# GpSimd's low halves of the weights in instructions of 256 elements per partition

## What is computed

```python
def trunk_layer(x, cvec, p, lam_init, ctx):
    shift1, scale1, gate1, shift2, scale2, gate2 = modulation(cvec, p['w_ada'], p['b_ada'])
    h = rms_norm(x, p['norm1_w']) * (1 + scale1) + shift1
    (mq, mk, mv, mo, mg, nq, nk, nv, dq, dk, dv, sz, sxbc, sdt, gpre) = split_cols(h @ p['w_in'])
    ...
    br = jnp.stack([a_out, b_out, c_out, d_out], axis=2)
    gates = jax.nn.sigmoid(gpre.reshape(B, S, N_BRANCH, D_MODEL))
    mixed = jnp.sum(gates * jnp.einsum('bsnc,ncd->bsnd', br, p['w_branch']), axis=2)
    x = x + gate1 * (mixed @ p['w_out'])
    h2 = rms_norm(x, p['norm2_w']) * (1 + scale2) + shift2
    x = x + gate2 * expert_choice_ffn(h2, p['w_router'], p['w_gate'], p['w_up'], p['w_down'])
```

## Time and profile before

| what | us |
|---|---|
| timed runs | 2199.38, 2208.94, 2211.12 |
| their median | 2208.94 |
| the profiled execution | 2198.71 |
| its span, first to last instruction | 2196.9 |
| GpSimd busy, 234 instructions | 455.8 |
| of that the low halves of L610, 164 instructions | 364.8 |
| VectorE busy, 1239 instructions | 662.9 |
| TensorE matmuls, 9096 | 1831.2 |

### The profile page before, as it was taken

One profiled execution on the slowest core, in us unless ns is written; L12 is line 12 of the kernel. 1 busy time (PEld: TensorE's weight loads), 2 busy tenths in 40 slices (PEclk: granted clock), 3 DMA queues, 4 the chain that ended last, 5 costly groups with the idle time before them and its releaser, 6 DMA issues.

```text
span 2196.9 us, 21970 instructions
## 1 busy us (share of the span) xinstructions
PE 1831.2 (83%) x9096; PEld 1169.9 (53%) x9096; DVE 662.9 (30%) x1239; ACT 545.7 (25%) x1054; POOL 455.8 (21%) x234
## 2 busy tenths in 40 slices
PE   5995988988988788888879879899686977888887
PEld 2885877877742222222358767777685422222223
DVE  2065334558320001011144452446584000110111
ACT  4432333221431111011144323322123310111111
POOL 0645322326200000000045452223271000000000
PEclk8998988978999999999989988889798999999999
DMA  9435243235479999999963424324323699999996
GB/s 353 106 115 197 99 147 114 99 97 186 157 305 407 428 425 427 428 427 428 394 195 119 153 108 142 132 91 163 108 87 153 260 429 427 427 428 429 427 427 293
DMA packets 119650, 567.72 MB, mean 258 GB/s; under 512 B 21376, under 2 KB 30848, under 8 KB 94464
## 3 DMA queue, kind: packets, MB, share of 16 engines
q1 hardware_dynamic: 108768, 543.91, 62.3%
q10 hardware_dynamic: 9920, 20.84, 2.7%
q0 software_dynamic: 864, 1.58, 0.3%
HBM read 550.57 MB, written 15.73 MB: 258 GB/s over the span
## 4 chain that ended last, share of the span: by engine, by line
PE 43%; DMA 35%; DVE 14%; ACT 3%; POOL 2%; issue 2%; SPq 1%; ACTq 0%; DVEq 0%
PE banks L678 19%; DMA ring<-in_w_down 11%; PE banks L1177 10%; DMA ring<-in_w_gate 10%; DMA ring<-in_w_up 10%; PE banks L995 2%; DVE work L1706 2%; DMA ring<-in_w_branch 1%; POOL small L624 1%; PE banks L684 1%; DMA ring<-in_w_ada 1%; DMA ring<-in_w_in 1%; PE banks L1147 1%; ACT work L1274 1%; DVE work L2075 1%
## 5 line engine op out<-in xcount | busy, mean ns | idle before, releaser
L1177 PE MATMUL banks<-ring,work 128*64 128x512 f32 x3072 | 703.3, 601 | 161.8 <-DMA ring<-in_w_gate 67.4
L610 POOL TENSOR_TENSOR ring_fp32r<-ring,ring_fp32r 128x1024 fp32r<-128x1024 f32 (+1 forms) x164 | 364.8, 2237 | 961.3 <-ACT ring_fp32r L1274 961.2
L1177 PEld LDWEIGHTS banks<-ring,work 128*64 128x64 f32 x3072 | 211.9, 137 | 615.8 <-issue 338.5
L678 PE MATMUL banks<-xT_fp32r,ring_fp32r 128*128 128x384 f32 x1280 | 367.9, 361 | 35.9 <-POOL ring_fp32r L610 32.6
L1274 ACT ACTIVATE work<-banks 32x512 f32<-32x512 f32 (+6 forms) x404 | 205.1, 528 | 458.4 <-PE banks L1177 253.4
L678 PEld LDWEIGHTS banks<-xT_fp32r,ring_fp32r 128*128 128x128 f32 x1280 | 251.0, 202 | 48.3 <-issue 39.1
L678 PE MATMUL banks<-hT_fp32r,ring_fp32r 128*128 128x384 f32 x640 | 225.4, 352 | 0.0
L1274 ACT ACTIVATE ring_fp32r<-ring 128x1024 fp32r<-128x1024 f32 (+1 forms) x164 | 156.4, 971 | 227.7 <-PE banks L678 161.9
L2129 DVE SCALAR_TENSOR_TENSOR xT<-banks,mod,xT 128x128 f32<-128x128 f32 (+1 forms) x128 | 46.9, 413 | 446.3 <-PE banks L1211 445.9
L678 PE MATMUL banks<-work_fp32r,ring_fp32r 128*128 128x384 f32 x768 | 149.1, 354 | 21.4 <-DVE work L2073 14.5
L678 PEld LDWEIGHTS banks<-work_fp32r,ring_fp32r 128*128 128x128 f32 x768 | 141.1, 198 | 27.6 <-DVE work L2073 11.4
(11 more groups left out here) (279 smaller groups left out, 1653.7 us busy)
## 6 DMA issues: line engine op xcount, KB each, us to landing
ring<-in_w_gate SPq DMA_DIRECT2D x64, 2048.0 KB, 12.2
ring<-in_w_up SPq DMA_DIRECT2D x64, 2048.0 KB, 12.8
ring<-in_w_down SPq DMA_DIRECT2D x64, 2048.0 KB, 13.6
ring<-in_w_in SPq DMA_DIRECT2D x28, 2048.0 KB, 9.4
ring<-in_w_ada SPq DMA_DIRECT2D x24, 2048.0 KB, 8.8
gates_spill<-work ACTq DMA_DIRECT2D x48, 192.0 KB, 3.9
work<-gates_spill ACTq DMA_DIRECT2D x16, 576.0 KB, 3.8
ring<-in_w_branch SPq DMA_DIRECT2D x4, 2048.0 KB, 14.7
```

Of the source, the lines that this page charges most:

```text
L610: ins = pool.tensor_tensor(rounded(w), w, rounded(hi), ALU.subtract)
L678: mm = pe.matmul(dst, a_, b_, start=(first and i == 0), stop=(last and i == 2))
L1177: mm = pe.matmul(dst[64 * hf:64 * hf + 64, :], x(k), w[:, kk, 512 * hf:512 * hf + 512], start=(k == 0), stop=(k == KC - 1), tile_position= ...
```

## The change

`low_parts` no longer gives a quarter to GpSimd in one instruction (or two, for the branch weights). A new function cuts it into pieces of 256 elements per partition, and each has an instruction of its own. Only the last of a quarter signals `lo_ready`, as before. Nothing else changes.

```diff
+            def pieces(w, hi):
+
+                rows, cols = w.shape[1], w.shape[2]
+                if cols == 512:
+                    return [(w[:, i:i + 1, c:c + 256], hi[:, i:i + 1, c:c + 256]) for i in range(rows) for c in (0, 256)]
+                n = 256 // cols
+                return [(w[:, i:i + n, :], hi[:, i:i + n, :]) for i in range(0, rows, n)]
+
             for l in range(L):
                 def low_parts(until):
...
                         pool.wait_ge(sem["hi_ready"], NQ * l + q + 1)
                         for w, hi in quarter(q):
-                            ins = pool.tensor_tensor(rounded(w), w, rounded(hi), ALU.subtract)
+                            for w_, hi_ in pieces(w, hi):
+                                ins = pool.tensor_tensor(rounded(w_), w_, rounded(hi_), ALU.subtract)
                         ins.then_inc(sem["lo_ready"], 1)
```

## The result

| | kernel before | changed kernel |
|---|---|---|
| median of the timed runs | 2207.42 us (4 runs, 2199.38 to 2211.12) | 2173.13 us (4 runs, 2167.19 to 2178.66) |
| profiled execution, its span | 2198.71 us, 2196.9 | 2168.74 us, 2166.9 |

The ratio is 0.9849, 95% interval 0.9806 to 0.9892. The changed kernel was timed twice more beside other kernels: 0.9895 [0.9868, 0.9923] and 0.9877 [0.9851, 0.9903]. Weighted by their intervals the three give 0.988, 26 us less. Two timed runs of the experiments, one of the kernel before (4459.7 us) and one of e17 (2240.6 us), had a granted clock of 0.43 and 0.81 instead of 0.93 and are left out of all ratios.

A forecast was written before the change was run, and what follows sets the result against it. It took TensorE (43%) and weight DMAs (35%) to lead the chain, with VectorE (14%) held by GpSimd's long turns. Its terms summed to -9.2 us, from a 2208.9 us median to 2199.7 us, range 2179 to 2217.

The forecast's parts named there:

- (b): Long stall of L2044, layer 1: stays, behind 16 pieces instead of eight instructions, +1.4 us (-0.1 to +6.3).
- the stall goes: Rival: VectorE gets its turn between pieces even behind a DMA issue, layer 1 saves about 9 us; 2179 us, chance 0.15.
- (g): Attention, both layers: L1868 is held less, but most of it is paid later; -2.0 us (0 to -5).
- (e): Branch products, both layers: VectorE's three instructions wait for pieces only, a chunk takes 5.3 us; -5.0 us (0 to -10).
- (f): Layer 0, 488 to 494 us: four VectorE instructions each held by one piece, not a 512-element instruction; -1.5 us (0 to -2.2).
- (c): Convolution, both layers: 24 short turns cost VectorE nearly what six long ones did; -1.6 us (-7 to +17).
- (d): Scan of L1733, both layers: 2.25 us of waiting become one or two pieces; -1.6 us (0 to -3.8).
- dear piece: Rival: GpSimd's price per instruction, paid four times, makes a piece cost up to 1.01 us; +35, 2244 us, chance 0.12.
- (a): Three places where TensorE waits for a quarter of weights, each 0.38 us longer; +1.1 us (0 to +4.9).
- no turns between pieces: Rival: VectorE gets no turn between pieces, so each quarter is one turn of 2.80 us; 2224 us, chance 0.09.
- no gain at the end: Rival: what VectorE gains is taken by TensorE or ScalarE next in line; 2207 us, chance 0.14.

The follow-up runs named there:

- e17: Kernel before (whole low halves) with a memset and a wait on it on GpSimd behind the store of the scan state; ratio to before 0.9949.
- e4: Kernel before with the store of the scan state moved behind the low halves of the first four branch quarters; ratio to before 0.9966.
- e7: Changed kernel with four gate quarters made ahead of the key and value stores and the scan-state store behind four branch quarters; ratio to before 0.9864.
- e8: Kernel before, whole instructions, with four gate quarters made earlier and the scan-state store behind the first four branch quarters; ratio to before 0.993.
- e13: Changed kernel with the scan-state store moved behind the first four branch quarters; ratio to before 0.9899, median 2179.25 us.
- e15: Kernel before with pieces of 256 in the gate quarters alone and the scan-state store behind four branch quarters; ratio to before 0.9926, median 2184.85 us.
- e12: Changed kernel with the low halves of two output-projection quarters moved behind the last merged chunks; ratio to before 0.9866.
- e14: Changed kernel, unaltered, timed again beside other kernels; ratio to before 0.9895, median 2177.64 us.
- e2: Kernel before with pieces of 256 in the 32 gate quarters alone; ratio to before 0.9946.
- e10: Changed kernel with only the first instruction behind the scan-state store left whole at 512 elements, in each layer; ratio to before 0.9871.
- e18: Changed kernel, unaltered, timed once more beside other kernels; ratio to before 0.9877.
- e3: Kernel before with pieces of 256 in the 16 quarters of the branch products and output projection alone; ratio to before 0.9901.
- e9: Kernel before with only the first 512-element instruction behind the scan-state store cut into two of 256, in each layer; ratio to before 1.0005.
- e1: Kernel before with pieces of 256 in the 26 projection quarters alone; ratio to before 1.0008.

## Why the prediction was wrong

The stages over the profiles of kernels with the order unchanged (e4, e7, e8, e13 and e15 left out), whole low halves at that place against pieces of 256, in us, layer 0 and layer 1 (means, with the number of profiles):

| stage | whole | pieces | difference |
|---|---|---|---|
| start to convolution, layer 0 | 110.7 (5; 110.1 to 111.9) | 112.2 (8; 110.2 to 114.1) | +1.5 |
| convolution to L1761 | 71.0, 72.3 (4) | 69.5, 70.8 (7) | -3.0 |
| to the first attention | 49.1, 49.4 (5) | 50.4, 50.5 (8) | +2.4 |
| attention to L1905 | 139.8, 143.3 (5) | 138.1, 139.4 (8) | -5.7 |
| to L2044 | 116.6, 117.8 (5) | 116.0, 116.1 (8) | -2.3 |
| to the first branch product | 21.4 (8 places, 5 with the stall) | 16.5 (12 places, 2 with the stall) | -9.8 for both layers |
| branch products | 48.7, 48.7 (5) | 45.0, 45.0 (8) | -7.5 |

Together that is -24.4 us, near the 26 of the timed runs.

- **(b), the step that failed.** The prediction let the stall of L2044 stay and priced it at +1.4 us. With pieces it goes: where VectorE arrives 0.06 to 0.07 us into the issue it was held for the whole run in 5 of 5 places with whole low halves and in 0 of 8 with pieces. What is left with pieces are the executions in which the store is late (e12, e14). In the table's stage a place with the stall takes 23.7 us and one without 17.5 with whole low halves, 23.8 and 15.0 with pieces. So a stall of 10.4 us costs some 6 at the end of the stage, and the first pair's layer 1 gained 8.7, stall and short turns together. The rival "the stall goes", with about 9 us for it, gave 2179 us, the closest of all; its 0.15 was too little. The reason given against it, that seven boundaries had given VectorE nothing, took one place for a rule. The number of boundaries is not what decides: in e12 and e14 fifteen gave nothing either, and in e17 whole instructions let VectorE in after one. At the other place, L1815, the stall did stay and grew, as (b) has it for L2044, and cost nothing.
- **The base.** 2208.9 us was the median of three runs, two of which lay 10 us above the third, and the prediction let that stay. Over its 89 timed runs in all, the kernel before has a median of 2201.7 us, spread from 2188 to 2211. Of the 26.6 us between the forecast and the measured median about 7 are this base, 17 are the terms, and 2 the luck of the first batch.
- **(g), mis-sized.** -2.0 us for the attentions; measured -5.7, and -2.3 behind them (e2 as a whole: -12, 7 to 17). The prediction took the wait of L1868 as paid later by its neighbours. With pieces its mean falls by 445 ns, 10.7 us over 24, and about half reaches the end. The -10.9 of the first pair of profiles was luck: single profiles with pieces have 135.1 to 140.5 us in layer 0, and TensorE's mean granted clock there goes with it, 0.90 at 135.1, 0.885 at 136.5 to 136.7, 0.86 at 140.3 to 140.5. Some of the -5.7 is clock too: at 0.885 to 0.887 layer 0 takes 136.6 us with pieces (e10, e14, e18) and 138.3 with whole ones (e3, e9). Whether pieces raise the clock or it comes by chance is not shown.
- **(e), mis-sized.** -5.0, measured -7.5. The forecast chunk of 5.3 us took 5.0, and the last copy of VectorE comes 8.1 us a layer earlier instead of 4.4. The tail was under-priced: the last subtraction stands 4.3 us behind that copy, not 2.1, since it has another subtraction and four pieces ahead of it. Last copy and last subtraction, layer 0 of the changed kernel:

```profile
535.88 0.77 DVE L2088 CAST work_fp32r<-work 128x384 fp32r<-128x384 f32 x1
540.96 1.00 POOL L663 TENSOR_TENSOR work_fp32r<-work,work_fp32r 128x384 fp32r<-128x384 f32 x1
```

- **(f), mis-sized by 1 us.** -1.5; in layer 0, where no stall stands, the stage fell from 17.5 us (3 profiles) to 14.9 (5), -2.6.
- **(c) and (d)** are not on the path, so their -3.2 us was wrong in kind: VectorE gained more than forecast (a mean of 940 ns, not 1.2 us), and e1 shows no change of time (at most 0.1% faster). The convolution stage is 1.5 us a layer shorter, but e2, with whole projections, has 1.2 of it, and e1, with pieces there, 0.3. One sum of (c) is off too: at 1.01 us a piece it gives +13 us and not +17, so "dear piece" would be 2240 us instead of 2244.
- **(a)** +1.1; the stages that hold its three places are +3.9 longer, within its bounds of 0 to +4.9, though the first has more spread than difference. The price of a piece, 0.70 us, was right.

Of the other rivals, "dear piece" needed 0.79 us and got 0.70; "no turns between pieces" is refuted by the branch rows; "no gain at the end" holds for the projections alone.

The Trainium skill, SBUF — State Buffer (SBUF: two separate sides), says that the pair of ports which VectorE and GpSimd share is held for a whole instruction, and the loser blocks. Most rows here agree: in e4 L2044 took 2.05 us instead of 0.96 beside an instruction of 1.28 us. By that rule a stall would be no longer than one instruction; the rows of 11.35, 11.99 and 11.78 us differ, and the measurement decides.

What stays open is why it matters when VectorE arrives, and why pieces let it in at 0.07 us into the issue where whole instructions don't. The stall of e9 began 2.9 us behind the start of the issue, after two turns, so the table above is not the whole rule. The rule that the prediction quoted from the Trainium skill (GPSIMD Engine Reference, Instruction dispatch), that GpSimd's cores are not held together between instructions, would fit a stall that a wait behind the issue removes; no run here shows the cores apart.

## What to carry to other kernels

Read where a stalled instruction of VectorE begins against the neighbour's queue: one that is held for a whole run of GpSimd instructions behind a DMA issue could be freed here by letting that run wait for the issue, without shortening anything. Then look for what waits beside it: the stall of 14.97 us here was worth nothing. When instructions of GpSimd hold VectorE, cut them until GpSimd is as late as VectorE and no further (256 elements here; 128 gave back most of the gain). Before a stall is priced as "stays" or "goes", look for it at every place of the trace and in several executions, since a place where a few tenths of a microsecond decide is not told by one profile.

## What the runs showed of the hardware

- A subtraction on GpSimd of 128, 256, 512 and 1024 elements per partition takes about 0.42, 0.70, 1.26 and 2.42 us when VectorE is still.
- VectorE was shut out for 20 instructions of GpSimd in a row (14.97 us), 16 (11.99) or 8 (11.35) when it arrived during a DMA issue of GpSimd with the run of instructions 0.02 to 0.03 us behind it: always at 0.58 us into the issue or later, at 0.06 to 0.07 us in 5 of 5 places with instructions of 512 elements and in none of 8 with 256. With a memset and a wait between issue and run, or no issue, it had its turn after one or two instructions.
- Behind most stalls of VectorE TensorE's next stretch ran at the higher of its two clocks, which would give back part of the stall. From the first of the 24 products ahead of the branch sums to VectorE's first branch instruction it was 4.6 us at a clock of 1.00 (2.4 GHz) in six of the seven places with a stall, TensorE having been idle for 1.5 to 1.8 us ahead of them. Without a stall it was 5.9 to 7.3 us at 0.58 to 0.75, a mean of the two levels, in 21 of 22 places (e9 and the late stores left out), behind 2.9 to 4.6 us of idling. The exceptions (e2 layer 1 with a stall, 6.1 us; e18 layer 0 without, 4.6 us) leave the link likely and not shown. Windows (busy, granted clock, DMA share, GB/s), the changed kernel and then e14 with its stall:

```profile
492.00:498.10 6.10, 6.08 (x26) 0.72 1.03 408
```

```profile
504.10:508.70 4.60, 4.54 (x26) 1.00 0.96 336
```
